# Turning the first feed-forward's up-projection round: standing activations, streamed weights, and 32-lane block transposes on VectorE

## What is computed

```python
def rms_norm(x, gain):
    xf = x.astype(jnp.float32)
    y = xf * lax.rsqrt(jnp.mean(xf * xf, axis=-1, keepdims=True) + NORM_EPS)
    return (y * gain.astype(jnp.float32)).astype(x.dtype)
...
        h = h + y
        hn = rms_norm(h, norm_ffn[i])
        h = h + jnp.square(jax.nn.relu(hn @ ffn_w1[i])) @ ffn_w2[i]
        gate = jax.nn.sigmoid(rms_norm(h, norm_ple[i]) @ ple_w_gate[i])
```

## Time and profile before

| | |
|---|---|
| median of three runs | 2210.76 us |
| profiled execution | span 2209.0 us from its first to its last instruction; no time of its own beside that is listed |
| TensorE busy | 2197.2 us (99%) |
| VectorE, ScalarE, GpSimd busy | 1445.2 (65%), 1106.9 (50%), 550.7 us (25%) |
| granted TensorE clock | 0.999 of full speed over the span |
| weight DMA | 756 pieces, 3.3 us from issue to landing |

### The profile page before, as it was taken

How to read it: one execution, slowest core, us unless ns; L and a number is a source line. 1 busy time by engine, 2 the same in 40 slices (tenths; PEclk the granted TensorE clock), 3 DMA queues, 4 the chain that set the end, 5 groups by cost and what they waited for, 6 DMA issues and landing times.

```text
span 2209.0 us, 34195 instructions
## 1 busy us (share of the span) xinstructions
PE 2197.2 (99%) x11625; PEld 1878.9 (85%) x11625; DVE 1445.2 (65%) x1925; ACT 1106.9 (50%) x1654; POOL 550.7 (25%) x531
## 2 busy tenths in 40 slices
PE   9999999999999999999999999999999999999998
PEld 7888988888888888888888887888888888888887
DVE  6877765555664565555566667567785688756875
ACT  6445555453453454445455455565553455534553
POOL 3202220350240141053000033005540245403431
PEclk9999999999999999999999999999999999999999
DMA  7675335556555555556555653545555555555554
GB/s 254 232 230 163 115 128 204 170 190 208 191 190 192 189 189 192 186 192 193 187 185 179 227 171 135 193 160 188 195 188 196 192 183 192 189 195 192 186 209 149
DMA packets 118072, 414.21 MB, mean 188 GB/s; under 512 B 12896, under 2 KB 18048, under 8 KB 117472
## 3 DMA queue, kind: packets, MB, share of 16 engines
q1 hardware_dynamic: 111600, 401.37, 53.9%
q10 hardware_dynamic: 6384, 11.70, 1.7%
HBM read 409.29 MB, written 2.15 MB: 186 GB/s over the span
## 4 chain that ended last, share of the span: by engine, by line
PE 98%; DVE 1%; ACT 1%; issue 0%; DMA 0%; DVEq 0%; ACTq 0%
PE bank L486 33%; PE bank L494 17%; PE bank L543 7%; PE bank L545 7%; PE bank L544 7%; PE bank L1059 4%; PE bank L1060 4%; PE bank L1061 4%; PE bank L599 1%; PE bank L601 1%; PE bank L600 1%; PE bank L619 1%; PE bank L994 1%; PE bank L656 1%; PE bank L796 1%; PE bank L798 1%
## 5 line engine op out<-in xcount | busy, mean ns | idle before, releaser
L1100 DVE TENSOR_TENSOR wboth<-raw,wboth 128x1024 fp32r<-128x1024 f32 x756 | 982.2, 1302 | 607.8 <-ACT wboth L1802 607.1
L1802 ACT CAST wboth<-raw 128x1024 fp32r<-128x1024 f32 x756 | 790.9, 1049 | 711.5 <-PE bank L545 241.6
L486 PE MATMUL bank<-A,wboth 128*128 128x512 f32 x2928 | 705.1, 391 | 0.3 <-DVE wboth L1100 0.3
L486 PEld LDWEIGHTS bank<-A,wboth 128*128 128x128 f32 x2928 | 537.0, 188 | 104.6 <-issue 1.0
L494 PEld LDWEIGHTS bank<-A,wboth 128*128 128x128 f32 x2928 | 376.7, 191 | 14.8
L494 PE MATMUL bank<-A,wboth 128*128 128x256 f32 x2928 | 384.0, 283 | 0.0
L543 PE MATMUL bank<-wboth,H 128*128 128x512 f32 x576 | 224.6, 390 | 0.0
L545 PE MATMUL bank<-wboth,H 128*128 128x512 f32 x576 | 224.2, 389 | 0.0
L544 PE MATMUL bank<-wboth,H 128*128 128x512 f32 x576 | 224.1, 389 | 0.0
L2257 POOL TENSOR_TENSOR bias<-z,rs 128x256 f32<-128x256 f32 x64 | 75.7, 1182 | 481.2 <-DVE z L1131 391.6
L2257 POOL TENSOR_TENSOR PT<-z,rs 128x256 f32<-128x256 f32 x88 | 73.4, 835 | 465.4 <-DVE z L1131 464.8
(11 more groups left out here) (293 smaller groups left out, 2409.1 us busy)
## 6 DMA issues: line engine op xcount, KB each, us to landing
raw<-wstream SPq DMA_DIRECT2D x756, 512.0 KB, 3.3
bias<-bias_rows ACTq DMA_DIRECT2D x6, 512.0 KB, 5.4
x<-xrows ACTq DMA_DIRECT2D x1, 2048.0 KB, 10.0
bias<-grows ACTq DMA_DIRECT2D x2, 1024.0 KB, 6.1
out<-x SPq DMA_DIRECT2D x8, 256.0 KB, 2.1
x<-xT SPq DMA_DIRECT2D x7, 256.0 KB, 4.6
pA<-bias_rows ACTq DMA_DIRECT2D x2, 512.0 KB, 8.9
Sm<-grows ACTq DMA_DIRECT2D x1, 1024.0 KB, 5.8
```

Of the source, the lines that this page charges most:

```text
L486: last = nc.tensor.matmul(bank(j)[:, :], whi[:, s, cols(i)], moving(j, k), start=(k == 0), stop=(k == K - 1))
L1100: V.tensor_tensor(wlo[:, s, :], raw[:, s, :], whi[:, s, :].bitcast(F32), ALU.subtract).then_inc(lo_ready, 1)
L1802: C.copy(whi[:, s, :], raw[:, s, :]).then_inc(hi_ready, 1)
```

## The change

The up-projection of all four chunks becomes `rows_group`: blocks of `A` are loaded, weights stream. Its weights lie in the stream in the order of rows. The result is token by feature, so the norm is one number per partition and the Relu on ACT applies it while reading PSUM (`scale=nrs`), into `zrow` (the buffer of `z`, 128 tokens x 2 halves x 512 features). But `H` must be feature by token. VectorE turns it: 16 STREAM_TRANSPOSE instructions for a group of 512 features, each on 32 lanes and 256 elements (eight blocks of 32 x 32), into `tA`. ACT squares the four tiles into `H`'s high part, GpSimd squares and subtracts as before. Gone are the bank addition on VectorE, GpSimd's multiplication, and in chunk 0 the spreading of the norm. The weights, the splitting and the down-projection stay.

```diff
-    STAGES += [(f"ff{_c}", CH, 16), (f"fd{_c}", 8, CH)]
+    STAGES += [(f"ff{_c}", 8, 16), (f"fd{_c}", 8, CH)]
...
 # TensorE
+            def chunk(c):
+                ff, fd, o = chunk_at(c)
+                first = {0: lambda: turn_wo(3)} if is_chunk(c, 0) else {}
+                for f in range(4):
+                    rows_group(o * 64 + (PB[ff] + 8 * f), PB[ff] + 8 * f, o * 16 + (UB[ff] + 2 * f), UB[ff] + 2 * f, DT, A,
+                               lambda k: (a1_ready, k + 1), first if f == 0 else {})
+                for f in range(4):
+                    late = {2: lambda: turn_fd(f - 1)} if f and is_chunk(c, FF_CHUNKS - 1) else {}
+                    rows_group(o * 64 + (PB[fd] + 8 * f), PB[fd] + 8 * f, o * 16 + (UB[fd] + 2 * f), UB[fd] + 2 * f, CH, H,
+                               lambda k: (ff_ready, c * CH + (k + 1)), late)
...
 # VectorE
-                steps(column_norm(nvar, ssqA, nrs, 2))
-                diagonal(nrs)
+                column_norm(nvar, ssqA, nrs, 2).then_inc(frs_ready, 1)
+
+            def turn_quarter(i, dst, src):
+
+                rows = src[32 * i:32 * i + 32, :, :].rearrange("p t (d c) -> p d t c", c=P)
+                for j in range(4):
+                    cols = dst[32 * j:32 * j + 32, :, :].rearrange("p d (t c) -> p d t c", t=QT)
+                    last = V.transpose(cols[:, :, :, 32 * i:32 * i + 32], rows[:, :, :, 32 * j:32 * j + 32])
+                return last
+
+            def ff_turn(c, g, i0):
+
+                if i0 == 0:
+                    ff, _, o = chunk_at(c)
+                    dve.wait_ge(z_ready, o * 16 + (4 + UB[ff] + 2 * g + 2))
+                    if g or not is_chunk(c, 0):
+                        dve.wait_ge(ff_hi, c * CH + 4 * g)
+                        dve.wait_ge(ff_step, c * CH + 4 * g)
+                for i in (i0, i0 + 1):
+                    turn_quarter(i, tA, zrow).then_inc(ff_turned, 1)
...
+                for g in range(4):
+                    steps_of[8 * g + 8] = lambda g=g: ff_turn(c, g, 0)
+                    steps_of[8 * g + 9] = lambda g=g: ff_turn(c, g, 2)
...
 # ScalarE
+            def ff_relus(c, g):
...
+                act.wait_ge(piece_used, o * 64 + (PB[ff] + SLOTS + 8 * g + 8))
+                act.wait_ge(z_ready, o * 16 + (4 + UB[ff] + 2 * g))
+                if g or not is_chunk(c, 0):
+                    act.wait_ge(ff_turned, c * 16 + 4 * g)
+                else:
+                    act.wait_ge(z_used, 4 + ZB["ff0"])
+                    act.wait_ge(frs_ready, 1)
+                for t in range(QT):
+                    C.activation(zrow[:, t, :], psum[(UB[ff] + 2 * g + t) % 4][:, :], ACT.Relu, scale=nrs[:, t:t + 1]).then_inc(z_ready, 1)
+
+            def ff_squares(c, g):
+
+                act.wait_ge(ff_turned, c * 16 + (4 * g + 4))
+                for j in range(4):
+                    C.activation(part(H, 4 * g + j, 0), tA[:, j, :], ACT.Square).then_inc(ff_hi, 1)
...
+                for g in range(4):
+                    steps_of[8 * g + 7] = lambda g=g: ff_relus(c, g)
+                    steps_of[8 * g + 10] = lambda g=g: ff_squares(c, g)
...
 # GpSimd
-                with pool.Fori(0, 4) as it:
+                for g in range(4):
+                    pool.wait_ge(ff_turned, c * 16 + (4 * g + 4))
                     for j in range(4):
-                        i = c * 16 + it * 4 + j
-                        take(o * 24 + it * 4 + UB[ff], ZB["ff0"], j, mul(zr[:, j, :], rs[:, :]))
-                        pool.wait_ge(ff_relu, i + 1)
+                        i = c * CH + (4 * g + j + 1)
                         G.tensor_tensor(tB[:, j, :], tA[:, j, :], tA[:, j, :], ALU.mult).then_inc(ff_step, 1)
-                        pool.wait_ge(ff_step, i + 1)
-                        pool.wait_ge(ff_hi, i + 1)
-                        G.tensor_tensor(part(H, it * 4 + j, 1), tB[:, j, :], part(H, it * 4 + j, 0).bitcast(F32),
+                        pool.wait_ge(ff_step, i)
+                        pool.wait_ge(ff_hi, i)
+                        G.tensor_tensor(part(H, 4 * g + j, 1), tB[:, j, :], part(H, 4 * g + j, 0).bitcast(F32),
                                         ALU.subtract).then_inc(ff_ready, 1)
```

109 lines of the change are left out of this document (38 added, 71 removed).

## The result

The changed kernel takes 2217.27 us (median of eight runs, 2216.79 to 2218.43) for 2211.31 of the kernel before in the same comparison (eight runs, 2210.42 to 2212.10): a ratio of 1.0029, 95% interval 1.0020 to 1.0038. It is slower by 6.0 us. The prediction was 2209.8, with "the same" as likeliest and a range of 2202.0 to 2216.0; the time lies outside the range. What happened is its rival (c).

A forecast was written before the change was run, and what follows sets the result against it. TensorE, busy 99% of the span, was taken as the bound: 8.60 us saved in up-projections, 7.6 lost waiting for H, so -1.0: span 2208.0, time 2209.8 us, called the same; range 2202.0 to 2216.0.

The forecast's parts named there:

- rival (c): Slower: dearer turnings delay GpSimd's chain at each chunk's end; +13.8 us at 0.50 a turning, +39 at 0.60; chance 0.17.
- I take 0.36: VectorE's turnings of a group: assumed 0.36 us from start to start, between bounds of 0.21 and 0.60.
- the prediction's own formula: TensorE's wait for H in each chunk's down-projection: about 1.9 + 16 x (turning price - 0.36) us.
- TensorE's saving: Up-projections with A's blocks loaded: 6.12 us saved in three later chunks, 2.48 in chunk 0, 8.60 in all.
- that wait at 0.47 a turning: Every group: TensorE waits for weights only if a turning costs over 0.47 us, because VectorE's split comes late.
- The exclusion between GpSimd and the splits: Last group of each chunk: GpSimd and VectorE's splits block each other, adding 5.0 us to GpSimd's 6.5; 1.9 wait per chunk.
- six collisions: Waits in GpSimd's last-group chain behind splits d5 to d10, 0.7 or 0.9 us each, 5.0 together.
- the gap inside a tile: GpSimd's work on a tile of H: 0.28 us between its operations of 0.61 and 0.74, 1.63 a tile.
- The clock: TensorE's granted clock was taken to stay full; a fall after a pause would make the forecast wrong altogether.
- D: The price of one turning on VectorE, from start to start, in us; assumed 0.36.
- Rival (a): One collision less at a chunk's end, with turnings of 0.345 or less: wait 0.8 a chunk, -5.4 us, 2205.4; chance 0.22.
- (b): No wait for H in the down-projections, the exclusion being milder: the whole -8.6 us, 2202.2; chance 0.15.

The follow-up runs named there:

- the small turnings in their first order: The changed kernel with every turning cut in two, 32 of 128 elements per group, each group of lanes written twice in a row; 2232.3 us.

## Why the prediction was wrong

- **The step that failed** is "I take 0.36: the same number of elements, one source, and a little for blocks that must fill before they empty." A turning is 0.452 from start to start. The length that I took was about right (0.436 for 0.42), in part by luck, since on kept lanes it is 0.394. What failed is the overlap of 0.07, carried over from rows in which each instruction uses the same lanes as the one before; and what stands ahead of the prediction, that VectorE's next instruction starts a little before the end of the last one where nothing is waited for, holds only for such rows. Each turning writes other lanes, and then it starts only behind the end of the last: turnings are 0.33 to 0.37 apart on one set of lanes, 0.452 on changing ones. The form of the instruction was asked about (runs of 32, blocks that fill), the form of the sequence was not.
- **The size of the error** is in the prediction's own formula: 1.9 + 16 x (0.452 - 0.36) = 3.4 a chunk for 1.9. Measured 3.30 to 3.46, so 13.5 for 7.6. Plain additions at 0.431 fit it with 3.0, and turnings on kept lanes, at 1.5 us less a group, fall back to 1.9 and 0.8. That term alone makes 5.9 of the 7.4 between the forecast span of 2208.0 and 2215.4; the other 1.5 are the 1.0 that the up-projections lose again and the 0.5 of the product ahead of the last chunk. By itself the term would give 2209.8 + 5.9 = 2215.7, just inside the range; the 1.5 that the sum had at nothing carry the time out of it.
- **TensorE's saving** was right: half of the turnings show 8.5 of the 8.60. Of it 1.0 is lost again in the up-projections, at 0.1 a group in the later chunks. The prediction had set that wait at 0.47 a turning and named what would show it (idle time put down to the split). At 0.452 it is 0.1 us a group and at 0.431 nothing, so my estimate of the limit is 0.452 - 0.1 / 16 = 0.446: the weight load goes ahead of its product, and the second eight turnings start behind the end of a split, not 0.08 before it; the prediction had counted neither.
- **The exclusion between GpSimd and the splits** was right in kind and in size: six collisions as counted, and a chain of 11.3 for 11.55. Two terms in it were off and cancel in part: a collision costs 0.95 us on average where 0.83 was taken, and the gap inside a tile is under 0.1 for the 0.28 taken. Without the exclusion there is no wait (splits that read PSUM).
- **The product ahead of the last chunk** (+0.5) was not foreseen, and every run of the new form shows it. The first row group needs two banks at once, and the second is freed only by ScalarE's copy at L2060; a wait of 0.35 is put down to it.
- **The clock** stayed full, as forecast.
- **The rivals and chances.** Rival (c) is what happened, with its place (end of each chunk), its price and its point ("from D = 0.45 on the sum passes +4.4"). It had 0.17. What should have moved the chances is the Trainium skill's rule ("VectorE: DVE Perf Modes", section "Two Vector instructions with no wait between them"), which I had not weighed: by it no overlap may be counted here. From rows alone D would then have been the 0.42 of the earlier trace rows at least, with the sum at -8.60 + 4 x (1.9 + 16 x 0.06) = +2.8 before any price for the transposing itself, so inside "the same" but on its slow side. Rival (a), which needs turnings of 0.345, would have lost most of its 0.22; (b), which hangs on the exclusion, would have kept its own. The measured 0.452 puts the formula at +4.9.

## What to carry to other kernels

Price a run of short VectorE instructions by the distance between starts in a row that has the same sequence of lanes: instructions that each write to another group of 32 lanes than the one before cost their whole length, and sixteen of them make 0.1 us into 1.6. Where a consumer's chain is alternately held by another engine, the cure is fewer links behind the late step: the square moved ahead of the turning gave 13 us back (2217.3 to 2204.2). And a wait that is paid once per chunk for the last group does not exist in the others, so their work may be spread to leave the splits alone.

## What the runs showed of the hardware

- STREAM_TRANSPOSE of fp32 on 32 lanes x 256 elements: 0.394 long and 0.33 to 0.37 apart on kept lanes, 0.436 and 0.452 when the lanes written change. Of 128 elements: 0.303 long and 0.316 apart when they always change.
- A plain addition of the same shape is 0.416 long and 0.431 apart, on 128 lanes 0.420 and 0.334: 32 lanes are no cheaper than 128, and a transpose costs about what an addition does.
- Eight runs of 32 elements or one of 256: the same 3.59 to 3.62 us for eight.
- With GpSimd and the splits both always ready, they alternate: GpSimd's operations of 0.61 and 0.74 both become 1.6, whichever is next, and the split's 1.22 becomes about 1.5 (four in 6.08).
- Of sixteen waits of TensorE of 2.7 to 2.8 us, nine were followed by products 0.43 apart at a granted clock of 0.51, where 0.227 is usual; that makes 0.97 over the stretch of 99.25 us. Sixteen waits of 0.8 (the small turnings in their first order) and three waits of up to 1.6 at a chunk's start left it at 1.00.
